# Stored weight sums for six octets a pass in half 1's second feed-forward product, with a ring of seven raw tiles

## What is computed

```python
h = _rmsnorm(x, ln2_w[l])
u = jax.nn.relu(jnp.einsum("bsd,df->bsf", h, w_ff1[l]))      # "first product": 2048 -> 8192
x = x + jnp.einsum("bsf,fd->bsd", jnp.square(u), w_ff2[l])   # "second product": 8192 -> 2048
```

## Time and profile before

| | |
|---|---|
| Median of three runs | 1503.34 us (1501.15 to 1503.94) |
| Profiled execution | 1503.15 us, span 1501.3 us |
| TensorE matmul busy | 1494.2 us, 100% of the span |
| VectorE (DVE) busy | 1143.3 us, 76% |
| ScalarE (ACT) busy | 811.1 us, 54% |
| GpSimd (POOL) busy | 130.9 us, 9% |
| DMA | 345.37 MB, mean 230 GB/s |

### The profile page before, as it was taken

One profiled execution on the slowest core, in us unless ns is written; L12 is line 12 of the kernel. 1 busy time (PEld: TensorE's weight loads), 2 busy tenths in 40 slices (PEclk: granted clock), 3 DMA queues, 4 the chain that ended last, 5 costly groups with the idle time before them and its releaser, 6 DMA issues.

```text
span 1501.3 us, 19534 instructions
## 1 busy us (share of the span) xinstructions
PE 1494.2 (100%) x7450; PEld 1257.9 (84%) x7450; DVE 1143.3 (76%) x1362; ACT 811.1 (54%) x925; POOL 130.9 (9%) x169
## 2 busy tenths in 40 slices
PE   9999999999999999999999999999999999999999
PEld 7888888888888888888888888888888888888877
DVE  6877756878787877876666777778988566578978
ACT  6555444676664544544444544456655445466654
POOL 6000000000041100100000111110000111110000
PEclk9999999999999999999999999999999999999999
DMA  8878897745545444446799888766877656666874
GB/s 293 216 256 294 302 341 264 241 159 169 171 166 168 141 140 162 144 142 205 268 320 326 268 287 293 244 224 221 302 261 265 193 188 195 191 222 217 311 283 149
DMA packets 156889, 345.37 MB, mean 230 GB/s; under 512 B 8336, under 2 KB 8848, under 8 KB 153488
## 3 DMA queue, kind: packets, MB, share of 16 engines
q1 hardware_dynamic: 148960, 317.09, 62.9%
q0 software_dynamic: 6592, 25.17, 4.7%
q10 hardware_dynamic: 1264, 2.13, 0.4%
HBM read 317.11 MB, written 27.26 MB: 229 GB/s over the span
## 4 chain that ended last, share of the span: by engine, by line
PE 93%; DVE 3%; DMA 2%; ACT 0%; issue 0%; SPq 0%; ACTq 0%; DVEq 0%
PE banks L630 46%; PE banks L1006 16%; PE banks L1052 9%; PE banks L1009 8%; PE banks L1074 6%; DVE lo L2192 2%; DMA raw<-in_w_ff 2%; PE banks L646 1%; DVE t_sums L2223 1%; PE banks L903 1%; PE banks L912 1%; DMA raw<-w_sums 0%; PE banks L788 0%; PE banks L764 0%; PE banks L667 0%
## 5 line engine op out<-in xcount | busy, mean ns | idle before, releaser
L1574 DVE TENSOR_TENSOR lo<-raw,hi 128x1024 fp32r<-128x1024 f32 x383 | 472.0, 1237 | 251.1 <-ACT hi L1107 249.9
L1107 ACT ACTIVATE hi<-raw 128x1024 fp32r<-128x1024 f32 x383 | 404.5, 1059 | 444.0 <-PE banks L630 263.5
L630 PE MATMUL banks<-hi,st 128*128 128x512 f32 x1584 | 499.1, 396 | 0.0
L630 PEld LDWEIGHTS banks<-hi,st 128*128 128x128 f32 x1584 | 290.6, 189 | 55.8 <-DVE lo L1574 0.7
L1006 PE MATMUL banks<-st,hi 128*128 128x512 f32 x1024 | 321.6, 395 | 0.0
L630 PE MATMUL banks<-lo,st 128*128 128x512 f32 x792 | 309.4, 391 | 0.0
L1009 PEld LDWEIGHTS banks<-st,lo 128*128 128x128 f32 x1024 | 192.4, 188 | 45.4
L1524 ACT ACTIVATE hi<-raw 128x1024 fp32r<-128x1024 f32 x160 | 168.7, 1061 | 110.6 <-PE banks L1074 61.8
L2192 DVE TENSOR_TENSOR lo<-raw,hi 128x1024 fp32r<-128x1024 f32 x160 | 192.5, 1222 | 22.0 <-ACT hi L1524 16.9
L1009 PE MATMUL banks<-st,lo 128*128 128x256 f32 x1024 | 201.1, 278 | 0.0
L630 PEld LDWEIGHTS banks<-lo,st 128*128 128x128 f32 x792 | 149.2, 188 | 31.6
(11 more groups left out here) (311 smaller groups left out, 1650.4 us busy)
## 6 DMA issues: line engine op xcount, KB each, us to landing
raw<-in_w_ff SPq DMA_DIRECT2D x116, 1024.0 KB, 5.9
raw<-in_w_in SPq DMA_DIRECT2D x99, 1024.0 KB, 5.0
raw<-w_sums SPq DMA_DIRECT2D x24, 1024.0 KB, 5.1
raw<-in_w_out SPq DMA_DIRECT2D x16, 1024.0 KB, 7.7
early_sum<-in_w_ff SPq DMA_DIRECT2D x12, 1024.0 KB, 8.0
w_sums<-early_sum SPq DMA_DIRECT2D x12, 1024.0 KB, 9.5
late_sum<-in_w_ff POOLq DMA_DIRECT2D x12, 1024.0 KB, 7.2
w_sums<-late_sum POOLq DMA_DIRECT2D x12, 1024.0 KB, 5.8
```

The lines of the kernel that those rows point to most:

```text
L630: last = pe.matmul(acc[:, t], x_t, v[:, (i + more) % PIECES, kk, :], start=m == 0 and kk == 0 and a == 0, stop=m == n - 1 and kk == 1 and ...
L1107: act.activation(hi[:, (i + more) % PIECES], raw[:, i // 2 % RAW, 2 * (i % 2):2 * (i % 2) + 2, :], ACT.Copy)\
L1574: dve.tensor_tensor(lo[:, (i + more) % PIECES], raw[:, i // 2 % RAW, 2 * (i % 2):2 * (i % 2) + 2, :], hi[:, (i + more) % PIECES].bitcast(F ...
```

## The change

Half 1's second product gets LOCAL = () and STORED = (0, 2, 3, 4, 5, 6): six sevens and two plain octets a pass, and no weight difference is made inside it. The stored octets of half 1's first pass are the twelve early steps (they were three octets of each pass before); half 0's are still the twelve late ones; the six of half 1's second pass are twelve new steps, at the places `LAST_STEPS` beside half 1's first product, moved by POOL through two new buffers, `last`. These are at 182 and 196 KB, where octets 5 and 6 of half 1's hidden channels come to lie later, so ACT waits for the last stores (`late_stored`) at place 2 of group 6 and of group 7. In half 1's second product the ring has seven raw tiles, four in `raw` and three in `raw_more`, which lies in the room of `st`, the operand of the first product; its first three loads wait until all pieces of the first product are used. The addresses of half 1's octets move, some semaphores are shared, and `made_before` counts in the eight differences of half 0's four local octets. Half 0's second product and everything before it keep their instructions.

```diff
+RING = 7
-LOCAL = ((2, 5), (2, 5))
-STORED = ((0, 3, 6), (0, 3, 6))
+LOCAL = ((2, 5), ())
+STORED = ((0, 3, 6), (0, 2, 3, 4, 5, 6))
-STORED_OCTETS = [(half, np_, o) for half in (1, 0) for np_ in range(2) for o in STORED[half]]
+STORED_OCTETS = [[(half, np_, o) for np_ in range(2) for o in STORED[half]] for half in range(2)]
+STORED_OCTETS = STORED_OCTETS[1][:6] + STORED_OCTETS[0] + STORED_OCTETS[1][6:]
+LAST_STEPS = [6, 9, 12, 17, 20, 25, 28, 33, 36, 41, 44, 52]
...
+        raw_more = sb("raw_more", [P, RING - RAW, 4, N], F32, 72)
...
+            at = (100, 214, 114, 168, 128, 182, 196, 64) if half else (100, 128, 114, 168, 136, 182, 196, 214)
...
+        last = [sb(f"last_sum{n}", [P, 2, 2 * N], F32, (182, 196)[n]) for n in range(2)]
...
             def product_tile(half, i, np_, o, which):
-                t = tile_at(half, np_, o, which)
+                dst, done, _ = tile_place(half, np_, o, which)
                 if i < RAW:
                     sp.wait_ge(lo_ready, piece0(half) + 2 * i - 6)
+                elif half and i < RING:
+                    sp.wait_ge(piece_used, piece0(1) + PIECES)
                 else:
-                    octet_used(half, *tiles_of(half)[i - RAW])
+                    octet_used(half, *tiles_of(half)[i - (RING if half else RAW)])
...
-            for o in SEVENS[1]:
-                token_sums(1, o)
+            pool.wait_ge(piece_used, piece0(0) + HALF_PIECES[0] + PIECES)
+            sum_in(FIRST_STEPS)
+            sum_in(FIRST_STEPS + 1)
+            h = FIRST_STEPS
+            for g in range(OCTETS):
+                if g and g - 1 in SEVENS[1]:
+                    token_sums(1, g - 1)
+                while h < ALL_STEPS and LAST_STEPS[h - FIRST_STEPS] < 8 * g + 8:
+                    sum_out(h)
+                    if h + 2 < ALL_STEPS:
+                        sum_in(h + 2)
+                    h += 1
...
+                    if half and g == OCTETS - 3:
+                        late_stored(half, 0)
                     if g == OCTETS - 2:
                         late_stored(half, 1)
...
-                          None if half else lambda p, g=g: stored_sums(8 * (QF0 + g) + p))
+                          (lambda p, g=g: stored_sums(8 * g + p, last_now)) if half else
+                          lambda p, g=g: stored_sums(8 * (QF0 + g) + p))
```

More of the change, by code:

```diff
@@ L209, in build_block @@
         t_sums = [{n: sb(f"t_sums{half}_{n}", [P, 2, N], F32, at) for n, at in homes.items()}
-                  for half, homes in enumerate(({0: 160, 1: 164, 3: 210}, {0: 64, 1: 68, 2: 72, 3: 76}))]
+                  for half, homes in enumerate(({0: 160, 1: 164, 3: 210}, {}))]
         def place_u(half):
-            at = (100, 128, 114, 168, 136, 182, 196, 214)
+            at = (100, 214, 114, 168, 128, 182, 196, 64) if half else (100, 128, 114, 168, 136, 182, 196, 214)
             def one(name, o, part):
@@ L310, in tile_at, with tile_place @@
             return 4 * (QG1 + MORE_QUADS if half else QG0) + tiles_of(half).index((np_, o, which))
+        def tile_place(half, np_, o, which):
+            t = tile_at(half, np_, o, which)
+            if half == 0:
+                return raw[:, t % RAW], landed[t % RAW], 16 * (t // RAW) + 16
+            turn, slot = divmod(tiles_of(half).index((np_, o, which)), RING)
+            if slot < RAW:
+                return raw[:, slot], landed[slot], 16 * (QG1 + MORE_QUADS + turn) + 16
+            n = slot - RAW
+            return raw_more[:, n], ev[f"side_landed{n}"], SIDE_BEFORE[n] + 16 * turn + 16
         def seven(half, o):
@@ L316, in sums_before @@
             before = 2 * len(LOCAL[0]) * half + len(LOCAL[half]) * np_ + LOCAL[half].index(o)
-            return STORED_SUMS + 4 * before
+            return 3 * (ALL_STEPS if half else FIRST_STEPS) + 4 * before
         def weight_sum(half, np_, o, n):
@@ L323, in summed, with made_before, last_now @@
         def summed(h):
-            return (early if h < EARLY_STEPS else late)[h % 2]
+            return (early if h < EARLY_STEPS else late if h < FIRST_STEPS else last)[h % 2]
+        def made_before(h):
+            return 3 * h + (FIRST_LOCAL if h >= FIRST_STEPS else 0)
         def sums_now(at, after):
             return [h for h, step in enumerate(SUM_STEPS) if step + after == at]
+        def last_now(at, after):
+            return [FIRST_STEPS + n for n, step in enumerate(LAST_STEPS) if step + after == at]
         def source(half, np_, o, n):
@@ L337, in source @@
                 which, k = ((0, 0), (0, 2), (1, 2))[n] if o in LOCAL[half] else (n // 2, 2 * (n % 2))
-            t = tile_at(half, np_, o, which)
-            return raw[:, t % RAW, k:k + 2, :], landed[t % RAW], 16 * (t // RAW) + 16
+            tile_, sem_, value = tile_place(half, np_, o, which)
+            return tile_[:, k:k + 2, :], sem_, value
         def x1_part(np_, t, j):
@@ L377, in product_tile @@
                     src = w_2_v[:, k:k + 4, span(N * (2 * np_ + which), N)]
-                sp.dma_start(dst, src).then_inc(landed[t % RAW], 16)
+                sp.dma_start(dst, src).then_inc(done, 16)
             def octet_used(half, np_, o, which):
@@ L400, in sums_in @@
                 src = w_2_v[:, k:k + 3:2, span(2 * N * np_, 2 * N)]
-                sp.dma_start(early[h % 2][:], src).then_inc(ev[f"t_in{h % 2}"], 16)
+                sp.dma_start(early[h % 2][:], src).then_inc(ev[f"side_landed{h % 2}"], 16)
             def sums_out(h):
@@ L420, in _ @@
             sp.dma_start(x_tok[:, :, 0:D // 2], x_v[:, :, 0:D // 2]).then_inc(ev["x_left"], 16)
-            sp.dma_start(raw[:, 0, 0:1], w_in_v[:, 0:1, span(COL_SWA, N)]).then_inc(ev["w_first"], 16)
-            sp.dma_start(raw[:, 0, 1:2], w_in_v[:, 1:2, span(COL_SWA, N)]).then_inc(ev["w_second"], 16)
+            sp.dma_start(raw[:, 0, 0:1], w_in_v[:, 0:1, span(COL_SWA, N)]).then_inc(ev["side_landed2"], 16)
+            sp.dma_start(raw[:, 0, 1:2], w_in_v[:, 1:2, span(COL_SWA, N)]).then_inc(ev["side_landed3"], 16)
             sp.dma_start(raw[:, 0, 2:4], w_in_v[:, 2:4, span(COL_SWA, N)]).then_inc(landed[0], 16)
@@ L1495, in late_stored @@
             def late_stored(half, b):
-                if half == 0:
-                    act.wait_ge(ev[f"l_out{b}"], 8 * LATE_STEPS)
+                act.wait_ge(ev[f"l_out{b}"], 8 * ((ALL_STEPS if half else FIRST_STEPS) - EARLY_STEPS))
             def u_hi_step(half, g):
                 def plain():
-                    if g == OCTETS - 1:
+                    if half == 0 and g == OCTETS - 1:
                         late_stored(half, 0)
@@ L1636, in right_lo, with stored_sums @@
                 return step
-            def stored_sums(at):
-                for h in sums_now(at, 0):
+            def stored_sums(at, now=sums_now):
+                for h in now(at, 0):
                     b = summed(h)
@@ L1643, in stored_sums @@
                     if h < EARLY_STEPS:
-                        dve.wait_ge(ev[f"t_in{h % 2}"], 16 * (h // 2) + 16)
+                        dve.wait_ge(ev[f"side_landed{h % 2}"], 16 * (h // 2) + 16)
                     else:
```

30 lines of the change are left out of this document (15 added, 15 removed).

## The result

The changed kernel takes 1507.73 us (median of 12 runs, 1506.77 to 1510.19), the kernel before, beside it, 1503.12 (12 runs, 1501.15 to 1506.54). The ratio is 1.0032, 95% interval 1.0025 to 1.0040: slower by 4.6 to 4.8 us, where 1499.3 us, a gain of 3.9, was forecast. It lies above the range given (1498.0 to 1506.5). The profiled execution has a span of 1506.8 us, before 1501.3.

The account below looks back on a forecast made before the run. TensorE, 93% of the chain, was taken to bound the kernel. 1503.15 - 2.7 (matmuls) - 1.8 (halts) + 0.5 (twelve steps) = 1499.15 us profiled, median 1499.3; eight-in-ten range 1498.0 to 1506.5.

Parts of the forecast that it names:

- The matmuls: Half 1's second product: octet 4 becomes a seven in each pass, 12 fewer matmuls at 0.2267 us, 2.7 us saved.
- The halts at LOCAL octets: Half 1's second product: TensorE's halts at LOCAL octets go as the differences leave DVE's queue, 1.8 us saved.
- The ring covers five stored sevens in a row: Half 1's second product, octets 2 to 6: seven raw tiles cover transfers 2.6 us short after five, 7 us to spare.
- its price with the cover gone, 5.2 us: Half 1's second product: without the ring's cover, late tiles would cost 2.6 us a pass, 5.2 us.
- Tile 4: Start of half 1's second product: it waits for the first product's end, lands 5.2 us later, cost taken as 0.
- Rival 3: Half 1's second product: only the matmuls are saved, late tiles still halt TensorE in octets 2 to 6; 1500.6 us, chance 0.12.
- The twelve steps: Beside half 1's first product: loads, stores and subtractions of the second pass's sums nearly fit; cost 0.5 us.
- POOL's round: Half 1's first product, per group: 7.85 us plus two store landings; fits in 22.3 us if they average 7.2.
- rival 1: Half 1's first product: POOL's round too long at 8.3 us a landing, TensorE halts some 4.5 us; 1503.3 us, chance 0.24.
- the lead of 3.9: Half 1's first product: a load may be 3.9 us late before TensorE halts, as DVE's splits run ahead.
- Rival 2: Half 1's first product: DMA engines full at 335 of 376 GB/s asked, 9.8 us of halts; 1508.6 us, chance 0.18.
- the signs of being right: Next profile: 696 matmuls in some 158 us, second product starting by 1336, DVE's waits for `last_sum` loads under 4 us.

Follow-up runs that it names:

- e4: The changed kernel with octet 4 left plain, so five stored sevens a pass, and eight spread-out new steps in place of twelve; 1501.50 us, ratio 0.9992.
- e1: The changed kernel without its twelve new steps, pass 2 reading pass 1's sums (second pass's sums left out); 1499.58 us, ratio 0.9979.
- e2: The kernel of e1 with a ring of four raw tiles in place of seven; 1518.35 us, ratio 1.0106.
- e8: The kernel of e3 with the first loads of the three added raw tiles let go earlier, before the first product ends; 1498.07 us, ratio 0.9971.
- e6: The changed kernel with the twelve new stores issued on ACT's queue, two places after each step's place, POOL only loading; 1502.75 us, ratio 1.0002.
- e5: The changed kernel with POOL's token sums moved between a group's last store and the wait for its landing; 1513.07 us, ratio 1.0067.
- e3: The changed kernel with three buffers `last` in place of two, same transfers, bytes and places; 1499.21 us, ratio 0.9979.
- e7: The kernel of e3 with every new store issued a second time, to a spare tensor; 1552.41 us (2 runs), ratio 1.0333.

## Why the prediction was wrong

**The matmuls, -2.7 us: right.** 12 fewer, and the chain shows 47.60 us for 210.

**The halts at LOCAL octets, -1.8 us: right.** They are gone with the LOCAL octets; alone (e4) they are worth 1.4, and in e1 the whole product gained 4.5, the two terms' sum.

**The ring covers five stored sevens in a row: right. Its 7 us to spare and its price with the cover gone, 5.2 us: wrong.** Six tiles cost nothing, but five, an estimated 5.4 us less of lead (four pieces of 1.36), already 1.1. The tiles of after's second product landed in 7.1 to 8.6 us at the median, and one near its start in 14.5, not in 5.2. With four tiles e2 loses 19. Tile 4, taken as 0, costs 0.4 us: it lands 6.33 us after its issue, not 5.2, at the end of a stretch with full queues. e8 gets it back. Rival 3, halts in octets 3 to 6, falls with this.

**The twelve steps, +0.5 us: this is the step that failed; 9.3 measured.** The form of POOL's round, a fixed part and two landings, was sound; the landing was mis-sized. POOL issued loads at 1186.80 and 1287.60, eight steps or four rounds apart: 25.2 us a round. From a store's issue to the next load's these eight took 10.5 us on average, so with the 0.4 of handing over a landing took 10.1. I took 6.7 to 7.5, with 8.3 as the upper bound; over all twelve the stores' median is 9.5, their longest 12.3. The fixed part was too long in my sum, 5.0 us in place of 6.6 (7.85 less a quarter of 4.85, as three of the four rounds had token sums): the sums took 3.3 to 3.9, and POOL hardly waited for DVE. That error worked for the forecast and hid a part of the other. By the working of rival 1 rounds of 25.2 give 4 x 2.9 - 3.9 = 7.7 us of halts; the late starts of TensorE's five halts in the trace add up to 7.7 (idle 6.5, the rest in the matmuls beside each halt). That the two agree so closely is partly luck, as the lead of 3.9 is an estimate. A further 1.6 us went in a way that stands in none of my terms, half the clock after halts (below). 7.7 + 1.6 = 9.3, all that is missing.

Why the landing was mis-sized: both bounds came from stretches with about one step in 20 us. The denser of them had 8.3, and I went below it for a stretch that is denser still, because of the 5.1 of the sparse one. The bound from above wasn't one. A store behind the other step's load on the same queue lands in about 12 us (the two waits of 11.9 and 11.8); with the stores on ACT's queue none takes over 10.3 (e6). The rule of the Trainium skill that I weighed there and took to be spoken against by the 5.1 us (DMA: Bandwidth & Descriptors, Queues, rings and completion order: each DMA engine takes its queues in turn, packet by packet) pointed the right way: tiles too went from 5.2 to 9.2. That it explains the amounts is not shown.

And I had worked out POOL's round only, not the buffer's. For a buffer it is the subtractions, 3.7 us (1195.04 to 1198.71), the store's landing, the load's landing and two hand-overs of 0.4: it needs store and load to land in some 17.8 us together. After's medians make 16.7; the means of the four rounds, 10.1 and 7.6, leave nothing over for a store that has to wait for POOL, and the long ones make 21; one buffer took 27.0 us from 1195.04 to 1222.03 against the 22.3 of a group. e5 and e6 show that relieving POOL alone does not do: 23.6 us a round stay in e6.

**The rivals.** Rival 1 named the right mechanism and gave 1503.3, with the landing again too small (8.3 for 10.1; and its own 8.8 - 3.9 is 4.9, not 4.5). Rival 2 gave 1508.6, close to the 1507.7 measured, by the wrong mechanism: e3 moves what was asked, 374 of 376 GB/s over 100 us, without a halt. A time that fits is no evidence for a rival. Its signs fitted too: from 1200 to 1280 after shows shares of 0.89 to 1.03 at 327 to 359 GB/s, and tiles landed in 9.2 us, just as I had listed for it. Only the shares of the two stretches that lost most, 0.89 and 0.91, hinted at waits between transfers; it took e3 to decide. The Trainium skill (DMA: Bandwidth & Descriptors, Where 436 GB/s comes from) puts a core's share of HBM at about 358 GB/s; e3's five stretches lie above it, as three of the four in the earlier trace rows did.

Of the signs of being right, 696 matmuls in 158.5 us held; the second product's start (1344.5, not by 1336) and the waits under 4 us did not. Of rival 1's, DVE waits of 4 to 6 us came, though at places 20 (6.15) and 41 (4.40) and not at 28, 36 and 44. The range failed because it stopped halfway into rival 2, and rival 1 had no room above its 8.3 us.

Still open: how much of the landing time comes from reads meeting writes and how much from queues sharing the engines. e6 separates the queue only, its order together with its kind, and e7 mixes too much.

## What to carry to other kernels

Where a transfer's landing lets the next one go, work out the cycle of the buffer (work, store's landing, load's landing, hand-overs) and that of the engine that waits, with landing times of a stretch at least as dense, or with its longest and not its median; here 5 us became 9 to 12. If it comes near the period, another buffer can be worth more than reordering: here the same bytes, at 366 to 391 GB/s, then cost nothing. The ring lost 1 to 2 us with one tile too few and 19 with two, so try its depth rather than derive it.

## What the hardware showed beyond this

After TensorE's halts the granted clock fell. TensorE's timeline of after at 1298:

```profile
1293.08 0.73 PE L1041 MATMUL banks<-st,hi 128*128 128x512 f32 x2 [0.69 <-DVE lo L1610]
...
1295.29 0.63 PE L1041 MATMUL banks<-st,hi 128*128 128x512 f32 x2
...
1298.23 1.22 PE L1041 MATMUL banks<-st,hi 128*128 128x512 f32 x2 [2.09 <-DVE lo L1610]
...
1299.67 1.05 PE L1041 MATMUL banks<-st,hi 128*128 128x512 f32 x2
...
1301.96 0.63 PE L1041 MATMUL banks<-st,hi 128*128 128x512 f32 x2
```

Two stretches, columns as in the earlier trace rows:

```profile
1298.30:1301.50 3.20, 3.20 (x10) 2.72 (x11) 3.20 (x4) 0.00 (x0) 1.27 (x2) 0.50 0.95 291
1301.70:1303.70 2.00, 2.00 (x13) 1.75 (x12) 2.00 (x3) 0.79 (x1) 0.00 (x0) 1.00 0.89 252
```

The granted clock is 0.50 in the first, the 1.2 GHz level, after halts of 0.69 and 2.09 us in the 6 us ahead, and 1.00 in the second; a pair of matmuls takes 1.22 and 1.05 us in place of 0.63. Three steps of the pattern take 3.73 us (1298.23 to 1301.96) in place of 2.09, so 1.6 us beside the halts. After the halts of 1.43 at 1225 and 1.24 at 1249 the clock was 1.00 over the stretch. In e6 the clock stays at 1.00 after a halt of 0.85 and is 0.50 from 1263.9 to 1267.2, after one of 2.01 at 1262.46. In e5 a stretch with a halt of 3.1 us has a mean clock of 0.91, in e7 five stretches have 0.80 to 1.00: a halt can cost more than its length.

Operations of DVE lengthen beside POOL's token sums. Where POOL made its token sums one right behind the other, they took 3.3 to 3.9 us, and one operation of DVE beside them was held up: a split at 1187.01 took 3.74 us in place of 1.22, the splits of `u_lo` at 1237.51 and 1288.14 took 3.15 and 2.86 in place of 0.68 (after). In the kernel before the sums take 4.85 us, and the split beside them 1.63. What holds DVE is not shown.

The DMA engines moved 391 GB/s over 20 us and 389 over 55, in loads mixed with stores in the first case. With the twelve steps running, transfers of 1 MB landed in 7 to 11 us at the median, by kind, whether TensorE was held up (after) or not (e3).
